# The output projection's first two column tiles are begun over seven of eight feature tiles while the last pair of heads is being finished

## The reference

```python
h = modulate(x, norm_mix_g[l], sh_a, sc_a)
q_mla, c_kv, k_rope, na_q, na_k, na_v, gq, gk, gv = mixer_inputs(h, w_in[l], ...)
o_mla = ...   # 6 heads of latent attention
o_na  = ...   # 4 heads of neighbourhood attention
o_gqa = ...   # 6 heads of grouped-query attention
x = x + g_a * mix_out(o_mla, o_na, o_gqa, w_out[l])      # concat(...) @ w_out
x = x + g_f * swiglu(modulate(x, norm_ffn_g[l], sh_f, sc_f), w_gate[l], w_up[l], w_down[l])
```

## Time and profile before

| | us |
|---|---|
| median of 3 runs | 1939.73 |
| lowest and highest | 1936.31, 1939.87 |
| the profiled execution | 1939.57 |
| its span, first to last instruction | 1937.8 |

### The profile page before, as it was taken

One profiled execution on the slowest core, in us unless ns is written; L12 is line 12 of the kernel. 1 busy time (PEld: TensorE's weight loads), 2 busy tenths in 40 slices (PEclk: granted clock), 3 DMA queues, 4 the chain that ended last, 5 costly groups with the idle time before them and its releaser, 6 DMA issues.

```text
span 1937.8 us, 29320 instructions
## 1 busy us (share of the span) xinstructions
PE 1738.0 (90%) x11708; PEld 1668.6 (86%) x11708; DVE 1189.9 (61%) x2265; ACT 724.1 (37%) x1421; POOL 223.5 (12%) x242
## 2 busy tenths in 40 slices
PE   4699778888899999999989977888889999999997
PEld 3689667778899999999989966777789999999997
DVE  6998666783667767676652257678456444454444
ACT  2323765772422222112243367567334221221122
POOL 0000524330000000000010052533100000000001
PEclk9999798999899999999989979899999999999998
DMA  9474000004233443433122010000322222122201
GB/s 321 139 231 131 24 1 2 1 23 142 98 120 120 157 147 135 147 119 119 41 72 78 29 39 1 1 3 13 118 66 66 66 65 87 65 83 90 65 22 54
DMA packets 107913, 159.83 MB, mean 82 GB/s; under 512 B 4976, under 2 KB 85680, under 8 KB 107568
## 3 DMA queue, kind: packets, MB, share of 16 engines
q1 hardware_dynamic: 105024, 152.52, 23.8%
q0 software_dynamic: 640, 2.92, 0.6%
q10 hardware_dynamic: 2160, 3.23, 0.5%
HBM read 155.08 MB, written 3.57 MB: 82 GB/s over the span
## 4 chain that ended last, share of the span: by engine, by line
PE 72%; DVE 17%; ACT 6%; issue 3%; POOL 1%; ACTq 1%; POOLq 0%; DVEq 0%
PE ps L584 23%; PE ps L585 22%; PE ps L586 22%; DVE ps L1232 5%; DVE pT L1217 2%; DVE negmax L1434 1%; PE ps L791 1%; DVE K L1217 1%; PE ps L648 1%; DVE Q L1328 1%; PE ps L592 1%; DVE hT L1217 1%; DVE V L1217 1%; ACT pT L1117 1%; ACT K L993 1%
## 5 line engine op out<-in xcount | busy, mean ns | idle before, releaser
L584 PE MATMUL ps<-hT,gw 128*128 128x320 f32 x1408 | 436.9, 310 | 6.8 <-DVE hT L1217 6.8
L585 PE MATMUL ps<-hT,gw 128*128 128x320 f32 x1408 | 436.7, 310 | 0.0
L586 PE MATMUL ps<-hT,gw 128*128 128x320 f32 x1408 | 436.6, 310 | 0.0
L1296 DVE SCALAR_TENSOR_TENSOR x<-ps,mod,x 128x320 f32<-128x320 f32 (+2 forms) x576 | 211.9, 434 | 122.7 <-PE ps L586 119.6
L584 PEld LDWEIGHTS ps<-hT,gw 128*128 128x128 f32 x1408 | 265.9, 189 | 7.3 <-issue 7.3
L585 PEld LDWEIGHTS ps<-hT,gw 128*128 128x128 f32 x1408 | 265.8, 189 | 0.0
L586 PEld LDWEIGHTS ps<-hT,gw 128*128 128x128 f32 x1408 | 265.7, 189 | 0.0
L1522 DVE TENSOR_TENSOR mm<-sl,ps 128x320 f32<-128x320 f32 x88 | 42.8, 488 | 317.9 <-issue 185.3
L584 PE MATMUL ps<-act,dw 128*128 128x320 f32 x704 | 219.0, 311 | 2.7 <-DVE act L1217 2.7
L585 PE MATMUL ps<-act,dw 128*128 128x320 f32 x704 | 218.7, 311 | 0.0
L586 PE MATMUL ps<-act,dw 128*128 128x320 f32 x704 | 218.7, 311 | 0.0
(11 more groups left out here) (199 smaller groups left out, 3714.7 us busy)
## 6 DMA issues: line engine op xcount, KB each, us to landing
gw_raw<-in_w_gate SPq DMA_DIRECT2D x22, 1024.0 KB, 5.5
gw_raw<-in_w_up SPq DMA_DIRECT2D x22, 1024.0 KB, 8.0
dw_raw<-in_w_down SPq DMA_DIRECT2D x22, 1024.0 KB, 5.0
ada_w<-in_w_adaT SPq DMA_DIRECT2D x42, 512.0 KB, 6.0
ada_wf<-in_w_adaT SPq DMA_DIRECT2D x34, 512.0 KB, 6.9
wi_raw<-in_w_in SPq DMA_DIRECT2D x16, 912.0 KB, 5.9
ada_wq<-in_w_adaT SPq DMA_DIRECT2D x20, 512.0 KB, 4.1
wo_raw<-in_w_out SPq DMA_DIRECT2D x16, 512.0 KB, 4.3
```

Source lines behind the costliest of these rows:

```text
L584: pe.matmul(dst, lh, rh, start=start, stop=False, skip_group_check=True)
L585: pe.matmul(dst, lh, rl, start=False, stop=False, skip_group_check=True)
L586: return pe.matmul(dst, ll, rh, start=False, stop=stop, skip_group_check=True)
L1296: i = ve.scalar_tensor_tensor(out=x[:, o, c0:c1], in0=ps[:, banks + hf_, s0:s0 + c1 - c0], scalar=mod[:, l, part * KD + o, q:q + 1], in1=x ...
```

## The change

Slots 80 and 82 get an entry `WO` each: ACT and DVE split the weight tiles of `o` = 0 and 1 there and no longer behind the attention. Slots 82 and 84 get an entry `W` each, on PE: the first seven feature tiles of the two halves of `o` = 0, 21 matmuls each. Behind the last entry, PE does the same for the two halves of `o` = 1 and only then waits for all of `o_ready`. In the loop, `o` = 0 and 1 are left with feature tile 7 alone, 6 matmuls each. The PSUM banks of the projection move down by two (from 2 to 7 to 0 to 5), since banks 6 and 7 are still used by the attention. DVE adds the results of `o` = 0 and 1 to `x` one after the other, both behind the lo part of `o` = 2. Nothing changes in SP's program.

```diff
@@ schedule()
         order += extra[2 * n + 1]
+        if n in (5 * NH, 5 * NH + 2):
+            order.append(("WO", (n - 5 * NH) // 2))
+        if n in (5 * NH + 2, 5 * NH + 4):
+            order.append(("W", 0, (n - 5 * NH) // 2 - 1))
@@ tensor engine
+                def out_proj(o, j, k0, k1):
+
+                    if k0 == 0 and o < 2:
+                        pe.wait_ge(wo_ready, l * KD + o + 1)
+                        pe.wait_ge(exp_done, l * UNITS + UNITS - 1 + o)
+                    cols = slice(j * HALF, (j + 1) * HALF)
+                    for k in range(k0, k1):
+                        m = split_mm(ps[:, 2 * (o % 3) + j, 0:HALF], wo[:, o % 2, 0, k, :], wo[:, o % 2, 1, k, :],
+                                     hT[:, k, 0, cols], hT[:, k, 1, cols], k == 0, k == KD - 1)
+                    return m
...
+                    elif s[0] == "W":
+                        if s[2] == 0:
+                            pe.wait_ge(o_ready, l * 2 * NP + 2 * NP - 2)
+                        out_proj(s[1], s[2], 0, KD - 1)
...
+                out_proj(1, 0, 0, KD - 1)
+                out_proj(1, 1, 0, KD - 1)
                 pe.wait_ge(o_ready, l * 2 * NP + 2 * NP)
                 for o in range(KD):
                     pe.wait_ge(wo_ready, l * KD + o + 1)
                     if o >= 3:
                         pe.wait_ge(x_done, l * XD + 1 + o - 2)
                     for j in range(2):
-                        for k in range(KD):
-                            cols = slice(j * HALF, (j + 1) * HALF)
-                            m = split_mm(ps[:, 2 + 2 * (o % 3) + j, 0:HALF], wo[:, o % 2, 0, k, :], wo[:, o % 2, 1, k, :],
-                                         hT[:, k, 0, cols], hT[:, k, 1, cols], k == 0, k == KD - 1)
+                        m = out_proj(o, j, 0 if o >= 2 else KD - 1, KD)
                     m.then_inc(y_ps, 1)
@@ scalar engine
+                    elif s[0] == "WO":
+                        wo_split(s[1])
...
                 sc.activation(warm[:], eps[:], ACT.Sqrt)
-                for o in range(KD):
-                    sc.wait_ge(wo_in[o % 2], 16 * (l * (KD // 2) + o // 2 + 1))
-                    if o >= 2:
-                        sc.wait_ge(y_ps, l * XD + o - 1)
-                    sc.activation(wo[:, o % 2, 0], wo_raw[:, o % 2], ACT.Copy).then_inc(wo_hi, 1)
+                for o in range(2, KD):
+                    sc.wait_ge(y_ps, l * XD + o - 1)
+                    wo_split(o)
@@ vector engine
+                    elif s[0] == "WO":
+                        wo_lo(l, s[1])
...
-                for o in range(KD):
-                    ve.wait_ge(wo_hi, l * KD + o + 1)
-                    lo(wo[:, o % 2, 1], wo_raw[:, o % 2], wo[:, o % 2, 0]).then_inc(wo_ready, 1)
-                    if o >= 1:
-                        residual(l, l * XD + o, o - 1, 2 + 2 * ((o - 1) % 3), 2)
+                for o in range(2, KD):
+                    wo_lo(l, o)
+                    for r in (0, 1) if o == 2 else (o - 1,):
+                        residual(l, l * XD + r + 1, r, 2 * (r % 3), 2)
```

More of the change, by code:

```diff
@@ L1098, in _, with wo_split @@
                     sc.activation(qm[:, t, j * 288:(j + 1) * 288], ps[:, 4 + n % 3, 0:288], ACT.Copy).then_inc(qm_done, 1)
+                def wo_split(o):
+                    sc.wait_ge(wo_in[o % 2], 16 * (l * (KD // 2) + o // 2 + 1))
+                    sc.activation(wo[:, o % 2, 0], wo_raw[:, o % 2], ACT.Copy).then_inc(wo_hi, 1)
                 sc.wait_ge(qm_ps, l * 2 * NT + 2 * NT)
@@ L1316, in cached_keys, with wo_lo @@
                 lo(K[r, kb, 1, LAT:640], src, K[r, kb, 0, LAT:640])
+            def wo_lo(l, o):
+                ve.wait_ge(wo_hi, l * KD + o + 1)
+                lo(wo[:, o % 2, 1], wo_raw[:, o % 2], wo[:, o % 2, 0]).then_inc(wo_ready, 1)
             def misc_lo_part(l, what, g):
@@ L1506, in _ @@
                 add_square(l, 5)
-                residual(l, l * XD + KD, KD - 1, 2 + 2 * ((KD - 1) % 3), 2)
+                residual(l, l * XD + KD, KD - 1, 2 * ((KD - 1) % 3), 2)
                 add_square(l, 6)
```

## The result

The changed kernel takes 1950.33 us (median of 5 runs, 1947.61 to 1953.21); the kernel before, in the same comparison, 1938.34 us (1933.43 to 1939.87). The ratio is 1.006, 95% interval 1.0041 to 1.0078: it is slower, by 12.0 us or 8 to 15 us. The forecast was 1953.4 us, 13.7 us slower. The profiled execution has a span of 1948.5 us and took 1950.33 us.

A forecast was written before the change was run, and what follows sets the result against it. PE, busy 90% of the span, was taken as the bound, so its waits and clock count. Later o = 2 (6.1 + 2.4 us) plus half clock (5.2 us) gave 13.7 us on 1939.73, so 1953.4 us; range 1946.5 to 1958.0.

The forecast's parts named there:

- The W matmuls go onto the path whole: Between head 15's transpositions: two W entries of 3.1 us each fill no idle PE time, adding 6.2 us.
- The rival that they hide in PE's waits: Head 15's loop: W matmuls hidden whole, last pair ends as before; -0.3 us in all, 1939.4 us; chance 0.04.
- WO 0 holds up head 15's first tile: ACT and DVE at slot 80: the first split delays the lo part of head 15's tile 0 by 0.8 us.
- the attention ends 7.0 us later: Attention's end, each layer: 0.8 us from WO 0 plus 6.2 us from W; bounds 5.1 to 8.2 us.
- The transfer: Third weight tile, issued after the last pair: o = 2 begins 6.1 us later in layer 0, 2.4 us in layer 1.
- The 1 us of the bound: Third weight tile's landing: allowed to vary by 1 us either way in each layer.
- The clock: PE after idling before o = 2: 22 matmuls at half clock, 2.6 us a layer, 5.2 us in both.
- My sentence that a longer idle should not do less: PE before o = 2: idle longer than 4.18 us should cost at least the same half-clock stretch of 22 matmuls.
- Rival 1: PE behind o = 2's wait: clock not lost again, or only for a few matmuls; 8.5 us slower, 1948.2; chance 0.09.
- Rival 2: Projection: third tile landed when PE ends o = 0, so o = 2 begins 4.4 us earlier; 1930.9 us; chance 0.04.
- Rival 4: Attention loop and clock: loop out of step or clock down longer; 19 us slower, 1958.8 us; chance 0.06.
- The sum of the stretch: Attention's end through projection, both layers: transfer and clock terms, 6.1 + 2.4 + 5.2 = 13.7 us later.

The follow-up runs named there:

- r3_w_behind: The changed kernel with the W entries' 42 matmuls moved behind the attention's last multiplication, ahead of those of o = 1; 1936.65 us, ratio 0.9991.
- r1_third_first: The changed kernel with SP issuing the projection's third and fourth weight tiles before the feed-forward transfers; 1924.90 us, ratio 0.9943.
- r4_filler: The changed kernel with 60 (layer 0) and 45 (layer 1) extra PE matmuls, results unread, in front of o = 2; 1945.59 us, ratio 1.0042.
- r5_split_only: The changed kernel with only the splits in slots 80 and 82 kept; all 48 matmuls of each tile behind the last pair; 1934.02 us, ratio 0.9981.

## Why the prediction was right, and by how much each term was off

The direction, the mechanism and the range (1946.5 to 1958.0) held. The terms of the sum, one by one:

- **The W matmuls go onto the path whole** (6.2 us a layer). Right: 6.17 us by r3_w_behind. The rival that they hide in PE's waits has fallen.
- **WO 0 holds up head 15's first tile** by 0.8 us. Right in kind, 0.7 us in size: before, PE waited 0.28 us there, after 1.00 us. Together with the last: I said that the attention ends 7.0 us later. From the first landmark to SP's first transfer it is 446.52 - 428.67 = 17.85 us before and 452.84 - 428.14 = 24.70 us after, 6.85 us more.
- **The transfer.** o = 2 in layer 0 was to begin 6.1 us later and begins 4.8 us later (from 37.83 us behind the landmark to 42.64 us). The step that was off is the landing: I moved it along with its 16.6 us, and it took 15.6 us. In layer 1, 2.4 us was said and 2.6 us measured; that it came so close is partly luck, since the landing took 0.5 us more there (13.4 us to ACT's split, 12.9 before) and the attention's end and the split together 0.3 us less than I said. The 1 us of the bound was needed.
- **The clock.** It did fall, as said, but cost 3.8 us and not 5.2 us. I had counted all 22 slow matmuls of the row of before; after the longer idle fewer ran slowly, in layer 1 most of all:

```profile
1407.00:1411.00 4.00, 3.92 (x15) 3.92 (x16) 3.24 (x8) 1.21 (x2) 0.00 (x0) 0.52 0.44 131
1411.00:1416.00 5.00, 5.00 (x36) 5.00 (x35) 0.00 (x0) 0.00 (x0) 0.00 (x0) 1.00 0.36 105
```

There the clock was back after 4 us in place of 5.8 us. My sentence that a longer idle should not do less was wrong in this. From o = 2 to the norm it takes 44.46 or 44.47 us in both layers of r1_third_first and r4_filler and in layer 1 of r5_split_only, whose waits are 0.87 to 1.88 us. The other runs lose against this, by the idle before o = 2: 2.4 us after 3.68 us (r3_w_behind, layer 1), 2.6 us after 4.61 us (r5_split_only, layer 0), 1.35 us after 5.80 us (r3_w_behind, layer 0), 1.7 us after 8.75 us and 2.15 us after 10.95 us (the changed kernel). In these five places the loss does not grow with the idle.

- **Rival 1** (no loss of clock, or a short one: 8.5 us) fell by r4_filler and the ruler. The times alone, 8 to 15 us, do not exclude it.
- **Rival 2** (the cover works, 1930.9) named the right condition. When r1_third_first fulfilled it, the kernel came to 1924.90, and o = 2 began 4.6 us earlier than before in each layer, behind the first landmark; rival 2 said 4.4 us (its own terms, 459.5 + 1.09 + 1.37, give 4.5). From the changed kernel to this one it was 22.5 us by the prediction (1953.4 - 1930.9) and is 20.5 us by the ruler.
- **Rival 4** (more is lost, 19 us) fell: in the changed kernel the later waits of the loop are 0.28 and 0.50 us as before, the attention's end came 6.85 us later and not 8.2, and the clock was back sooner, not later, than before.

The sum of the stretch was said as 8.7 + 5.0 = 13.7 us and is 7.1 + 4.4 = 11.5 us.

## What to carry to other kernels

Before matmuls are moved ahead into a wait, look at what their time was hiding: here a transfer was ready 0.9 us before PE came to it in layer 0, and 12 us of the matmuls that hid it, put ahead of its issue or directly behind it, laid it bare. Work put between the steps of a loop that goes round several engines filled nothing here, since PE did not idle at that very place; and what the loop's end starts (here 4.5 MB of transfers in layer 0) was late by as much. Behind the loop, where the last copies run, a part of it did fill a wait. First issue the transfer that will be needed next. With the splits moved, the two together took the kernel from 1938.52 to 1924.76 us.

## What the runs showed of the hardware that I had not expected

**The same wait can cost the clock or not.** In block 0 of the feed-forward part of layer 0, PE waits 2.66 us for `act` in both kernels. Before:

```profile
555.26 0.64 PE L584 MATMUL ps<-act,dw 128*128 128x320 f32 x1 [2.66 <-DVE act L1217]
...
556.00:558.00 2.00, 2.00 (x9) 2.00 (x9) 1.94 (x2) 0.97 (x2) 0.00 (x0) 0.50 0.83 332
```

After:

```profile
561.72 0.41 PE L588 MATMUL ps<-act,dw 128*128 128x320 f32 x1 [2.66 <-DVE act L1239]
...
562.00:564.00 2.00, 2.00 (x15) 2.00 (x15) 1.55 (x3) 1.44 (x2) 0.00 (x0) 1.00 0.99 393
```

With half clock 9 matmuls are at work in 2 us, with full clock 15. From the norm's matmul of layer 0 (510.87 and 517.40) to the first of layer 1's input projection (1008.33 and 1012.17) the changed kernel took 494.77 us and the kernel before 497.46 us, 2.7 us less. In the next stretch, up to head 14's first tile of layer 1 (1360.57 and 1366.63), it took 354.46 against 352.24 us, 2.2 us more; where that comes from is not shown. So the two stretches nearly cancel. I have shown the change of clock for this one place; whether it makes up the 11 us between the lowest and the highest run of the kernel before is not shown.

**The landing varies by 1 us without a cause that I could find.** From SP's first transfer to ACT's start of the third tile in layer 0 it was 16.6 us in the kernel before, in r3_w_behind and in r5_split_only, 15.6 us in the changed one and 15.3 us in r4_filler. In layer 1, with one transfer less, it was 14.5 us in r3_w_behind, 13.4 us in the changed one, 12.9 us in r5_split_only and 12.8 us in r4_filler, so the kernels do not keep their order. It is not that PE is idle meanwhile: in r4_filler PE was busy nearly all that time. It stays open.
